# The sample's attention in a streaming encoder step: cached scores a step earlier, own scores a step later than them

## What is computed

```python
def diff_attend(q, q_pos, segments, lam):        # segments: cached (1024 keys), own (64 keys)
    scores = []
    for k, _, k_pos in segments:
        s = jnp.einsum('bqhmd,bkhmd->bhmqk', q, k) * scale
        ...
        scores.append(jnp.where(visible, s, -1e30))
    p = jax.nn.softmax(jnp.concatenate(scores, axis=-1), axis=-1)
    p = p[:, :, 0] - lam * p[:, :, 1]
    out = 0.0
    for k, v, _ in segments:
        out = out + jnp.einsum('bhqk,bkhe->bqhe', p[..., start:start + n], v)
        ...
...
of = of * lax.rsqrt(jnp.mean(of * of, axis=-1, keepdims=True) + RMS_EPS) * subln_g * (1.0 - lam_init)
return of.reshape(B, L, D_MODEL) @ w_o
```

## Time and profile before

| | |
|---|---|
| time, median of 3 runs | 2372.91 us (2372.08 to 2373.29) |
| profiled execution | 2374.91 us, its span 2373.0 us |
| share of TensorE busy | 96% |
| share of VectorE, ScalarE, Pool busy | 64%, 49%, 25% |
| mean granted clock of TensorE | 0.982 |

### The profile page before, as it was taken

How to read it: one execution, slowest core, us unless ns; L and a number is a source line. 1 busy time by engine, 2 the same in 40 slices (tenths; PEclk the granted TensorE clock), 3 DMA queues, 4 the chain that set the end, 5 groups by cost and what they waited for, 6 DMA issues and landing times. The chain is left out here.

```text
span 2373.0 us, 42348 instructions
## 1 busy us (share of the span) xinstructions
PE 2286.6 (96%) x17003; PEld 2244.4 (95%) x17003; DVE 1525.6 (64%) x2302; ACT 1157.8 (49%) x1947; POOL 583.4 (25%) x499
## 2 busy tenths in 40 slices
PE   8999999999998999999999999999999999899997
PEld 8989999999998898999999999999999999889997
DVE  6887768556787677444474566655677666465444
ACT  4445543555643556433354455655466554354332
POOL 2256501123310343111251123011252011132110
PEclk9999999999998999999999999999999999999999
DMA  9667675454675454654569655544556446345552
GB/s 234 171 182 221 188 213 184 120 168 134 191 223 156 125 172 142 187 151 145 147 179 292 181 160 172 154 124 135 149 152 183 132 146 187 109 146 161 146 151 82
DMA packets 702292, 391.11 MB, mean 165 GB/s; under 512 B 25001, under 2 KB 689042, under 8 KB 702098
## 3 DMA queue, kind: packets, MB, share of 16 engines
q1 hardware_dynamic: 662720, 332.44, 49.0%
q10 hardware_dynamic: 39378, 55.96, 7.1%
HBM read 366.53 MB, written 21.82 MB: 164 GB/s over the span
## 5 line engine op out<-in xcount | busy, mean ns | idle before, releaser
L468 DVE TENSOR_TENSOR wl<-raw,wh 128x1024 fp32r<-128x1024 f32 (+1 forms) x640 | 792.9, 1239 | 481.4 <-ACT wh L462 479.7
L484 PE MATMUL tile_ps<-xh,wh 128*128 128x256 f32 (+1 forms) x3520 | 1066.0, 303 | 25.6 <-DVE wl L468 13.0
L485 PE MATMUL tile_ps<-xl,wh 128*128 128x256 f32 (+1 forms) x3520 | 1048.3, 298 | 0.0
L486 PE MATMUL tile_ps<-xh,wl 128*128 128x256 f32 (+1 forms) x3520 | 1047.9, 298 | 0.0
L462 ACT CAST wh<-raw 128x1024 fp32r<-128x1024 f32 (+1 forms) x640 | 656.3, 1026 | 770.6 <-PE tile_ps L486 746.9
L484 PEld LDWEIGHTS tile_ps<-xh,wh 128*128 128x128 f32 x3520 | 674.1, 192 | 35.8 <-DVE wl L468 17.8
L485 PEld LDWEIGHTS tile_ps<-xl,wh 128*128 128x128 f32 x3520 | 675.4, 192 | 1.1 <-issue 0.2
L486 PEld LDWEIGHTS tile_ps<-xh,wl 128*128 128x128 f32 x3520 | 674.6, 192 | 0.0
L594 POOL TENSOR_TENSOR hl<-hf,hh 128x256 fp32r<-128x256 f32 (+1 forms) x176 | 252.5, 1435 | 1300.5 <-ACT hh L526 1300.0
L484 PE MATMUL tile_ps<-hh,wh 128*128 128x320 f32 (+1 forms) x1472 | 446.3, 303 | 19.5 <-POOL hl L594 18.7
L486 PE MATMUL tile_ps<-hh,wl 128*128 128x320 f32 (+1 forms) x1472 | 435.8, 296 | 0.0
(11 more groups left out here) (293 smaller groups left out, 1774.3 us busy)
## 6 DMA issues: line engine op xcount, KB each, us to landing
raw<-in_ffn_w_in_dram SPq DMA_DIRECT2D x352, 512.0 KB, 3.9
raw<-in_ffn_w_out_dram SPq DMA_DIRECT2D x128, 448.0 KB, 3.7
raw<-in_ffn_w_out_dram SPq DMA_DIRECT2D x64, 512.0 KB, 4.1
raw<-in_ssm_w_glu_dram SPq DMA_DIRECT2D x32, 512.0 KB, 3.9
raw<-in_attn_w_kv_dram SPq DMA_DIRECT2D x32, 512.0 KB, 3.9
wt<-scr_w ACTq DMA_DIRECT2D x16, 512.0 KB, 4.2
cp<-scr_c ACTq DMA_DIRECT2D x16, 512.0 KB, 3.7
raw<-in_attn_w_q_dram SPq DMA_DIRECT2D x16, 512.0 KB, 4.1
```

The lines of the kernel that those rows point to most:

```text
L468: nc.vector.tensor_tensor(wl[n % WS][:, 0:k, :], raw[n % RAWS][:, 0:k, :], wh[n % WS][:, 0:k, :].bitcast(F32), ALU.subtract).then_inc(w_lo, 1)
L484: nc.tensor.matmul(o, wh[w][:, kk, :], xa, start=kk == 0, stop=False)
L485: nc.tensor.matmul(o, wh[w][:, kk, :], xb, start=False, stop=False)
L486: mm = nc.tensor.matmul(o, wl[w][:, kk, :], xa, start=False, stop=kk == ROWS[n] - 1)
```

## The change

The own scores become a function of their own, `own_scores`, and so do the own maximum and what is computed from both, `own_maxima`. They stand in step B of their head, TensorE's ahead of the folds. The exponentials of a head go from step B to step C on ScalarE. SAMPLE goes from 34 to 33, so head k has A in step 34 + 3k, B in 35 + 3k, C in 36 + 3k. After the last head the third yield is left out on the three engines, so what follows is issued in the same step 60. ScalarE gets an additional root of one column in front of the wait for the last sum of squares.

```diff
@@ pe_sample @@
                 mm.then_inc(z_sc, 1)
+
+            def own_scores(h):
+                b = h % 2
                 if h == 0:
                     pe.wait_ge(s_sq, 2 * ITEMS - 1)
                 wait(pe, z_fin, h - 1)
...
                 if k < NH:
                     scores(k)
                 yield
+                if k < NH:
+                    own_scores(k)
                 if k:
                     folds(k - 1)
                 yield
...
-                yield
+                if k < NH:
+                    yield
@@ dve_sample @@
                 V.reduce_max(st[:, 0:1], misc[:, 0:2, :].rearrange("p c n -> p (c n)"), axis=AX.X).then_inc(z_big, 1)
+
+            def own_maxima(h):
+                st = stz[:, h % 2]
                 dve.wait_ge(z_own, h + 1)
...
                 yield
+                if k < NH:
+                    own_maxima(k)
...
-                yield
+                if k < NH:
+                    yield
@@ act_sample @@
                     copied(k - 1)
-                if k < NH:
-                    exps(k)
                 if k + 2 < NH:
                     act.wait_ge(z_sc, k + 1)
                     act_load_k(act, k + 2)
                 yield
+                if k < NH:
+                    exps(k)
                 if k:
                     evict(k - 1)
...
-                yield
+                if k < NH:
+                    yield
+
+            A.activation(small[:, 9:10], small[:, 0:1], ACT.Sqrt)
             act.wait_ge(z_sq, NH)
...
-        SAMPLE = 2 * ITEMS + 2
+        SAMPLE = 2 * ITEMS + 1
```

## The result

| | before | after |
|---|---|---|
| time, median | 2373.1 us (2372.1 to 2373.5) | 2444.1 us (2443.2 to 2449.2) |
| span of the profiled execution | 2373.0 us | 2441.2 us |
| mean granted clock of TensorE | 0.982 | 0.972 |

The change makes the kernel slower, by a ratio of 1.0298 with a 95% interval of 1.0286 to 1.0310: 71.0 us. 2435 was forecast, with 2407 to 2452 as the range. One execution of a later kernel (fill_c, 2986.5 us, mean granted clock 0.70) fell into the chip's slow state and stands in no comparison.

A forecast was written before the change was run, and what follows sets the result against it. TensorE, busy for 96% of the span, was taken as the bound. Waits 43.2, clock 18.6 and start and end 0.4 sum to 62.2 us, giving 2435 us on the median's base, with 2407 to 2452 as the range.

The forecast's parts named there:

- Which waits, how many: TensorE's folds in step B and output in step C wait for work of the same step, 7 times each.
- Their length: TensorE's waits: 22.8 us in step B plus 21.9 in step C, less 1.5 of old waits, together 43.2 us.
- Clock, the number of falls: TensorE's clock falls to 1.2 GHz behind 12 of the 14 new waits.
- Clock, the size of the term: Each fall on TensorE lasts 3.4 us and loses 1.55 us; 12 falls give 18.6 us.
- the bound of 43 us for long stretches: Upper bound of TensorE's clock term: 14 falls, each twice as long, 14 x 2 x 1.55 us.
- The start: Head 0's cached scores one step ahead find their data ready: 0; VectorE's wait in step 35: 0 to 1.
- The end: Last head: pTS wait goes, eviction behind wl of tile 60 costs 0.2 us, added root 0.2; together +0.4 us.
- The table at step 39: Output's wait at step 39: exponentials' table load between cast and exponential adds 1.28 us, making 4.0 us.
- 2416: Rival: TensorE's clock doesn't fall, since folds, output and transposes lie close around each wait; 2416 us, chance 0.13.
- 2459: Rival: TensorE's clock stays low from wait to wait, 43 us instead of 18.6; 2459 us, chance 0.09.
- 2405: Rival: only one of the two waits, folds or output, binds; 2405 us, chance 0.07.
- 2371: Rival: both waits covered, TensorE not bounding this stretch, old waits of 1.5 us go; 2371.4 us, chance 0.03.

The follow-up runs named there:

- fill_c: Changed kernel with 22 unread matmuls ahead of each of the 7 waits of output only: 2439.2 us, ratio 1.0269.
- Experiments 1 and 2: Changed kernel with own scores and maxima back in step A: 2407.1 us; changed kernel with exponentials of heads 1 to 7 back in step B: 2415.9 us.
- experiment 3: Changed kernel with own scores and maxima back in step A and exponentials of heads 1 to 7 back in step B: 2374.9 us, ratio 1.0005.
- experiment 4: Changed kernel with unread matmuls in the waits, 24 ahead of each wait of folds and 22 ahead of each of output: 2417.9 us, ratio 1.0186.

## Why the prediction was right, point by point

- **Which waits, how many.** Right: the folds for the last maximum operation and the output for the exponentials, 7 times each, and no other of weight. Experiments 1 and 2 take them away one by one, and experiment 3 shows that nothing else of the change costs anything.
- **Their length.** Right: 22.0 us are listed in step B for 22.8 forecast, 21.0 in step C for 21.9. The forecast went by the starts of the matmuls, and on that scale it is 23.4 and 22.2. The points of VectorE and ScalarE relative to a tile's end are the same in both kernels, which is why rows of before could price waits that it does not have. In the output tiles the wait for the folds was put at 3.05 us with weights of 896 columns and at 3.3 with 1024; measured by the starts are 3.03 and 3.27 (heads 2 and 3; listed as 2.83 and 3.07). One reading was wrong and did no harm: the listed wait of 0.3 us in the earlier trace rows is not that of the folds at 1973.69, which have no wait in their row, but of those at 2017.05 (0.33 us there). At 1973.69 the last matmul of the tile had started at 1973.31, so that TensorE was ready at 1973.43 by its pace of 0.12 us. The prediction has 1973.39, and its 3.3 us stand.
- **Clock, the number of falls.** Right: 12 stretches for 12 forecast, behind 14 waits. That it is just 12 is luck in part, since 12 was a choice between 9 and 14 and nothing told which two would be missing. The 16 of 17 waits on which it rested are those of one execution; in the profiled execution of the changed kernel 5 of the 17 other waits of 1.75 us and more have no slow stretch (they last 1.9 to 2.4 us).
- **Clock, the size of the term.** This is the step that was off, and it makes up the 9 us between 2435 and 2444. I gave each fall 3.4 us at the low level, by the row of a single wait in the earlier trace rows. Measured are 65 us in 12 stretches, 5.4 on average, since 6 of the 7 behind the folds' waits last 6.8 us. That is 28.0 us by the ledger, and 27 by experiment 4, instead of 18.6. It is above the 21.7 us (14 falls at 1.55) that the forecast's own range had room for. The terms of that range add up to 2425 to 2443, not 2446, and the measured 2444 is just outside them; only the bound of 43 us for long stretches, and with it the wider range, holds it. The rows of before could have told more: I looked at what follows the wait in the row at 939.4, which is dense, and did not ask what follows it here, which is the folds. What the Trainium skill says in "TensorE: Matmul & The Clock Gate", HAM oscillation, that a wait in each pass brings the slow clock back in each pass, agrees with the after trace in 12 of 14 cases.
- **The start.** Right: 0 was forecast, and experiment 3 shows none. The new wait of the scores for the exponentials of head 0, 0.3 us, I had not listed.
- **The end.** Right in kind: the 0.8 us wait for pTS went, and VectorE's wl of tile 60 was next. Output starts at 2112.92, the eviction at 2115.30, 2.4 us behind it (2.5 forecast). In all the end got 0.15 us longer where 0.4 was forecast: from the end of tile 60 to the projection's first matmul 9.56 us, plus 1.95 for the folds that moved ahead, against 11.36. The additional root costs 0.1, not 0.2.
- **The table at step 39.** The wait of head 1 was 4.0 us as forecast. With the drain that the Trainium skill gives in "ScalarE: Activation LUTs", What ACT_TABLE_LOAD costs, it would have been 5.4 by estimate. The trace shows no drain there: the exponential starts 1.30 us after the load (1952.32 to 1953.62).
- **The rivals.** The clock did fall (against 2416); it did not stay low from wait to wait (against 2459): in the stretch 2004.3 to 2011.3 it is at 1.00. Both waits bound (against 2405), and they were not covered (against 2371).

## What to carry to other kernels

In an order written out by hand, cover is counted in steps: a wait in step s for another engine's work in step s - 1 costs little (at most 1.2 us here), and the same wait for work of step s costs all that stands ahead of it in that engine's step, here cast and wl, about 3 us. When an operation is moved by a step, go through everything that waits for its semaphore, also the waits that the diff does not show. And price a wait of TensorE twice, once for its length and once for the slow clock behind it; the second price depended here on what follows the wait.

## What was unexpected of the hardware

At the same length of about 3 us, a wait followed by narrow matmuls (16 of 64 columns, then a tile) was followed by 6.8 us or more at 1.2 GHz in 16 of 21 cases (three kernels), one followed by wider ones (16 of 128 columns, then a tile) in 2 of 21, by 3.4 us in 15 and by none in 4. Putting 16 matmuls of 256 columns behind the first kind of wait, 13 us of work in all, cost nothing that can be told, and filling the waits with 322 useless matmuls took 27 us off the changed kernel.
